# A decoder layer with a mixture of experts on one core: a second gather buffer at expert 0, and the last expert's rows added by TensorE

## The reference

```python
out, new_a, new_b, v = token_mixer(x, ...)
h = layer_norm(ALPHA * x + out, ln1_g, ln1_b)
# moe_ffn(h): router, then
for e in range(N_EXPERTS):                       # 16 experts, 1024 -> 512 -> 1024
    u = jax.nn.silu(t @ w_gate[e]) * (t @ w_up[e])
    out = out + gates[:, e:e + 1] * (u @ w_down[e])   # gates: 2 non-zero per token
y = layer_norm(ALPHA * h + f, ln2_g, ln2_b)
```

## Time and profile before

| | us |
|---|---|
| median of 3 runs | 1049.32 (1045.19 to 1050.66) |
| the profiled execution | 1048.14 |
| its span, first to last instruction | 1046.4 |
| mean granted TensorE clock | 0.978 |
| TensorE busy | 995.1 (95%) |
| VectorE busy | 792.4 (76%) |
| ScalarE busy | 473.1 (45%) |
| GpSimd busy | 372.4 (36%) |
| moved by DMA | 190.52 MB, mean 182 GB/s |

### The profile page before, as it was taken

How to read it: one execution, slowest core, us unless ns; L and a number is a source line. 1 busy time by engine, 2 the same in 40 slices (tenths; PEclk the granted TensorE clock), 3 DMA queues, 4 the chain that set the end, 5 groups by cost and what they waited for, 6 DMA issues and landing times.

```text
span 1046.4 us, 19478 instructions
## 1 busy us (share of the span) xinstructions
PE 995.1 (95%) x7212; PEld 901.5 (86%) x7212; DVE 792.4 (76%) x965; ACT 473.1 (45%) x665; POOL 372.4 (36%) x275
## 2 busy tenths in 40 slices
PE   7999999999999999999999999995999999999980
PEld 7999999999999998999999999974677777777760
DVE  2698889888999995744434598147789898999986
ACT  4232222323232244334442323424678787878763
POOL 2444434444544770445454544410110000000362
PEclk9999999999999999999999999997899999999995
DMA  7433232323232221333235534548899999999574
GB/s 220 122 93 95 85 100 81 100 80 100 81 101 81 80 82 49 100 110 89 81 99 170 172 90 144 208 163 317 300 368 391 375 391 379 383 388 393 203 253 165
DMA packets 163400, 190.52 MB, mean 182 GB/s; under 512 B 6675, under 2 KB 114195, under 8 KB 163340
## 3 DMA queue, kind: packets, MB, share of 16 engines
q1 hardware_dynamic: 156619, 177.65, 49.8%
q0 software_dynamic: 3008, 10.55, 3.2%
q10 hardware_dynamic: 3729, 1.75, 0.7%
HBM read 179.16 MB, written 11.76 MB: 182 GB/s over the span
## 4 chain that ended last, share of the span: by engine, by line
PE 57%; issue 25%; POOL 12%; DVE 3%; DMA 2%; ACT 1%; POOLq 0%; DVEq 0%
PE pr L986 27%; PE pr L1172 16%; POOL w_lo L562 12%; PE work L1172 8%; PE work L1148 1%; DMA hs<-h_rows,ids 1%; PE work L1069 1%; PE pr L1198 1%; DVE w_gate_lo L1625 1%; PE pr L1088 1%; PE work L1191 1%; DMA y_b<-y_rows,slot_b 1%; DVE y_a L1793 0%; PE work L1096 0%; DVE y_b L1789 0%
## 5 line engine op out<-in xcount | busy, mean ns | idle before, releaser
L562 POOL TENSOR_TENSOR w_lo<-raw,w_hi 128x512 fp32r<-128x512 f32 x208 | 298.0, 1453 | 334.5 <-ACT w_hi L680 334.5
L986 PE MATMUL pr<-x_hi,w_hi 128*128 128x260 f32 x1264 | 255.0, 283 | 0.2 <-POOL w_lo L562 0.2
L986 PE MATMUL pr<-x_hi,w_lo 128*128 128x260 f32 x1264 | 254.7, 283 | 0.0
L986 PE MATMUL pr<-x_lo,w_hi 128*128 128x260 f32 x1264 | 254.3, 283 | 0.0
L684 ACT ACTIVATE ev<-pr 128x520 f32<-128x520 f32 x96 | 58.1, 605 | 375.1 <-PE pr L986 375.1
L986 PEld LDWEIGHTS pr<-x_hi,w_hi 128*128 128x128 f32 x1264 | 195.0, 189 | 0.5 <-POOL w_lo L562 0.4
L986 PEld LDWEIGHTS pr<-x_hi,w_lo 128*128 128x128 f32 x1264 | 195.0, 188 | 0.0
L986 PEld LDWEIGHTS pr<-x_lo,w_hi 128*128 128x128 f32 x1264 | 194.4, 188 | 0.0
L1355 DVE SCALAR_TENSOR_TENSOR work<-b_pad,par,work 128x512 f32<-128x512 f32 x224 | 148.2, 743 | 0.0
L680 ACT ACTIVATE w_hi<-raw 128x512 fp32r<-128x512 f32 x208 | 118.9, 623 | 4.9 <-DMA raw<-in_w_in_dram 2.6
L599 POOL DMA_INDIRECT hs<-h_rows,ids x16 | 20.2, 1260 | 256.4 <-DVE ids L1619 246.6
(11 more groups left out here) (337 smaller groups left out, 1704.5 us busy)
## 6 DMA issues: line engine op xcount, KB each, us to landing
raw<-in_w_in_dram SPq DMA_DIRECT2D x80, 512.0 KB, 3.7
w_gate<-in_expert_w_gate_dram SPq DMA_DIRECT2D x16, 2048.0 KB, 14.9
w_up<-in_expert_w_up_dram SPq DMA_DIRECT2D x16, 2048.0 KB, 14.3
w_down<-in_expert_w_down_dram SPq DMA_DIRECT2D x16, 2048.0 KB, 13.6
y_rows<-y_out SPq DMA_DIRECT2D x15, 384.0 KB, 13.1
raw<-in_w_a_out_dram SPq DMA_DIRECT2D x8, 512.0 KB, 3.6
raw<-in_w_c_out_dram SPq DMA_DIRECT2D x8, 512.0 KB, 3.7
raw<-in_w_b_out_dram SPq DMA_DIRECT2D x8, 512.0 KB, 3.6
```

Source lines behind the costliest of these rows:

```text
L562: pool.tensor_tensor(w_lo[:, slot, k], raw[:, slot, k], w_hi[:, slot, k].bitcast(F32), ALU.subtract).then_inc(w_split, 1)
L986: mm = pe.matmul(pr[slot][:, h, 0:HALF], w[:, slot, k, :], x[:, k, h * HALF:(h + 1) * HALF], start=(k == 0 and w is w_hi and x is hi), sto ...
```

## The change

Two edits that had been made apart are joined.

*At expert 0.* A second buffer `hs_second` takes the gather of expert 1's rows (`gather_second`), which waits for the row numbers alone; `turn` reads it once. Gate of slot 2 is loaded ahead of `h_out`, and "up" of slot 2 and "down" of slots 1 and 2 are held back until the second gather has landed. 30 idle transposes stand ahead of TensorE's wait for `mb`; `keep_busy` issues 18 and 8 in place of 20 and 12.

*At the end.* `share_marks` makes a 96x128 matrix for each block of 128 tokens: the weight of the last expert's row for each token that has one. TensorE transposes it between the two halves of the last "down", and `share_last` computes, in PSUM, `y_a` (times the identity, float32) plus this matrix times the last expert's rows, in three products of parts. ScalarE and VectorE split the matrix and the rows. `slot_ready` sends a token whose second expert is the last to another row, with weight `s_wm` zero. GpSimd so fetches `y_b` after all stores of `y_out`, and only the samples wait for the last halves. `summed_up` adds `y_b` in PSUM. For blocks 0 to 2 the final pass is split: ScalarE scales (`scaled`), GpSimd adds the bias row (`shifted`) and the block leaves from `y_b`; block 3 is finished by VectorE in two halves and sent by ScalarE. The branch is turned round, so that the path taken stands first, with its own copy of the end.

```diff
@@ SyncE, before expert_pass
             expert_load(first, 0, TURN[0], "down")
+            expert_load(first, 2, TURN[2], "gate")
             h_out()
-            expert_load(first, 2, TURN[2], "gate")
+            sp.wait_ge(second_in, 16)
             expert_load(first, 2, TURN[2], "up")
-            sp.wait_ge(first.gathered, 16)
             expert_load(first, 1, TURN[1], "down")
             expert_load(first, 2, TURN[2], "down")
@@ GpSimd
+            def gather_second():
+                pool.wait_ge(first.ids_ready, 3)
+                pool.indirect_dma_start(out=hs_second[:], out_offset=None, in_=h_rows,
+                                        in_offset=bass.IndirectOffsetOnAxis(ap=ids[:, 1:2], axis=0)).then_inc(second_in, 16)
+            def shifted():
+                for b in range(3):
+                    pool.wait_ge(std2_ready, (5, 8, 11)[b])
+                    pool.tensor_tensor(y_b[:, b, :], y_a[:, b, :], ln2_rows[:, 1, :], ALU.add).then_inc(added, 1)
-                pool.wait_ge(first.half_stored, 32)
-                fetch(y_b, slot_b, y_b_in, y_rows[0:E * C, :])
+                pool.wait_ge(slots_ready, 4)
+                pool.wait_ge(first.stored, 16 * E)
+                fetch(y_b, slot_ready, y_b_in, y_rows[0:(E - 1) * C, :])
+                pool.wait_ge(first.half_stored, 32)
+                fetch_samples(sy_b, 2, y_b_in, y_rows[0:E * C, :])
+                shifted()
@@ ScalarE, last_rows_out
                     act.activation(y_last[:, cols], work[0][0:C, h, :], ACT.Copy).then_inc(ps.half_ready, 1)
+                    if ps is first:
+                        if h == 0:
+                            act.wait_ge(end_mm, 2)
+                            act.activation(share_hi[:], pr[1][0:C, 1, :], ACT.Copy).then_inc(end_act, 1)
+                        act.activation(y_last_hi[:, cols], work[0][0:C, h, :], ACT.Copy).then_inc(end_act, 1)
@@ ScalarE, the end
+            def scaled(b):
+                act.wait_ge(var_ready, (3, 5, 7)[b])
+                act.activation(y_a[:, b, :], y_a[:, b, :], ACT.Copy, scale=agg[:, b % 2, 3:4]).then_inc(std2_ready, 1)
+                deviation(0)
+                deviation(1)
+                scaled(0)
...
+                deviation(2)
+                scaled(1)
...
+                deviation(3)
+                scaled(2)
@@ TensorE
+            for _ in range(30):
+                pe.transpose(pr[0][:, 1, 0:P], ident[:], ident[:])
             pe.wait_ge(mb_ready, 1)
...
-                    keep_busy(20)
+                    keep_busy(18)
                 turn(ps, n0)
                 if ps is first:
-                    keep_busy(12)
+                    keep_busy(8)
...
+                down_last(ps, t, 0)
+                if ps is first:
+                    pe.wait_ge(end_dve, 3)
+                    for b in range(4):
+                        mm = pe.transpose(pr[1][0:C, 1, b * P:(b + 1) * P], share_tok[:, b, :], ident[:])
+                    mm.then_inc(end_mm, 1)
+                down_last(ps, t, 1)
+                    pe.matmul(z_tile[b][:, h, :], ident[:], y_a[:, b, cols], start=True, stop=False)
+                    for w, y in ((share_hi, y_last_hi), (share_lo, y_last_hi), (share_hi, y_last_lo)):
+                        mm = pe.matmul(z_tile[b][:, h, :], w[:, n], y[:, cols], start=False, stop=y is y_last_lo)
@@ VectorE
+                do(dve.tensor_tensor(share_tok[:], share_tok[:], rep(s_wb[:, 0:4], 2, C), ALU.mult), to_end)
...
+                partial(0, landed)
+                dve.wait_ge(end_act, 1)
+                dve.tensor_tensor(share_lo[:], pr[1][0:C, 1, :], share_hi[:].bitcast(F32), ALU.subtract).then_inc(end_dve, 1)
+                share_low(0)
+                partial(1, landed)
+                share_low(1)
+                partial(2, landed)
```

More of the change, by code:

```diff
@@ L511, in _, with results_out @@
             expert_pass(first, 0, 0)
+            def results_out():
+                for b in range(2):
+                    sp.wait_ge(added, b + 1)
+                    sp.dma_start(y_prompt[0, b * P:(b + 1) * P, :], y_b[:, b, :]).then_inc(fin_out[0], 16)
+                sp.wait_ge(fin_ready, 1)
+                sp.dma_start(y_sample[:, 0, :].rearrange("s (c f) -> (s c) f", f=CS), sy_a).then_inc(fin_out[0], 16)
+                sp.wait_ge(added, 3)
+                sp.dma_start(y_prompt[0, 2 * P:3 * P, :], y_b[:, 2, :]).then_inc(fin_out[0], 16)
             n_max = further_passes(sp)
-            with sp.If(n_max > C):
+            with sp.If(n_max < C + 1):
+                results_out()
+            with sp.Else():
                 sp.wait_ge(first.stored, 16 * E)
@@ L530, in _ @@
                 sp.sem_inc(y_read, 1)
[L531 to L540, removed]
+                results_out()
+            sp.wait_ge(fin_out[0], 64)
             sp.wait_ge(fin_out[1], 32)
@@ L606, in step @@
                     t = e + n0
-                    if m == 0:
+                    if m == 0 and ps is first:
+                        gather_second()
+                    elif m == 0:
                         gather(ps, 1, t + 1)
@@ L663, in _ @@
                 fetch_samples(sy_b, 2, y_b_in, y_rows)
-            with pool.Else():
-                pool.wait_ge(first.stored, 16 * E)
-                pool.wait_ge(first.half_stored, 32)
-                fetch(y_b, slot_b, y_b_in, y_rows[0:E * C, :])
-                fetch_samples(sy_b, 2, y_b_in, y_rows[0:E * C, :])
+                shifted()
         @block.scalar
@@ L1143, in find_ids, with turn @@
                 mm.then_inc(ps.ids_mm, 1)
-            def turn(ps, t):
-                pe.wait_ge(ps.gathered, t * 16 + 16)
+            def turn(ps, t, second=False, late=16):
+                source = hs
+                if second:
+                    source = hs_second
+                    pe.wait_ge(second_in, 16)
+                else:
+                    pe.wait_ge(ps.gathered, t * 16 + late)
                 for k in range(KB):
-                    mm = pe.transpose(work[0][:, k // 4, k % 4 * C:(k % 4 + 1) * C], hs[:, k * P:(k + 1) * P], ident[0:C, 0:C])
+                    mm = pe.transpose(work[0][:, k // 4, k % 4 * C:(k % 4 + 1) * C], source[:, k * P:(k + 1) * P], ident[0:C, 0:C])
                 mm.then_inc(ps.turned, 1)
@@ L1223, in step @@
                     if m < 15:
-                        turn(ps, t + 1)
+                        turn(ps, t + 1, second=ps is first and m == 0, late=0 if ps is first else 16)
                     product(ps, "up", s, t, x_hi_t, x_lo_t, lambda h: pr[0][0:C, 1, :], 1)
@@ new lines, in partials, with partials_late @@
+            def partials(landed):
+                dve.wait_ge(back_in, 32)
+                partial(0, landed)
[5 more added lines that the diff above has]
+                partial(2, landed)
+            def partials_late():
+                partial(3, 16)
+                sample_partial(16)
@@ L1758, in _ @@
             expert_pass(first, 0)
-            dve.wait_ge(back_in, 32)
-            partials(16)
+            counts = (chain.n, to_var.n, to_fin.n, to_slots.n)
             n_max = further_passes(dve)
-            with dve.If(n_max > C):
+            with dve.If(n_max < C + 1):
+                dve.wait_ge(ln_in, 16 * 2 * (TS + 1))
+                results(partials_late)
+            chain.n, to_var.n, to_fin.n, to_slots.n = counts
+            with dve.Else():
                 dve.sem_inc(further.ids_ready, 1)
                 dve.sem_inc(further.u_ready, 1)
+                partials_late()
                 dve.wait_ge(first.half_ready, 2)
```

233 lines of the change are left out of this document (152 added, 81 removed).

## The result

| | median, us | runs | ratio to before | 95% interval |
|---|---|---|---|---|
| kernel before, same chip | 1046.72 | 10 | 1 | |
| changed kernel | 1052.16 | 10 | 1.0046 | 1.0030 to 1.0062 |
| changed kernel, second series | 1052.27 | 12 | 1.0033 | 1.0018 to 1.0048 |

The profiled execution took 1052.15 us, its span 1050.4 us (before: 1048.14 and 1046.4). The forecast was -1.6 us against the profiled execution; +4.0 came. The time lies inside the range that I gave, but a slight gain was forecast and a small loss was measured: both intervals lie above 1.

The account below looks back on a forecast made before the run. Bound: the chain through the second gather, then TensorE with DMA nearly full, then the tail. Start and experts 5.9 + 0.3 - 2.5 - 3.1 - 1.1 = -0.5, tail 2.1: 1.6 us gained, median 1047.7 us, range 1041.0 to 1053.5.

Parts of the forecast that it names:

- the range that I gave: Whole kernel: measured time between 1041.0 and 1053.5 us.
- a slight gain: Whole kernel: 1.6 us off the profiled execution, to 1046.5 us; 1047.7 us as median.
- a stretch in which the tie had hardly begun: Expert stage: three intervals up to 977 us gave steps of 18.17 us, costing 3.1 us over 11 stores.
- the slack: Expert stage: 2.05 us before TensorE needs VectorE's low part of `u`, called the tightest; TensorE then loses 2.5 us.

Follow-up runs that it names:

- second profile: The profile of the whole change run once more, unaltered; that series measured 1.0033 of the kernel before (1052.27 us).

## What to carry to other kernels

Before bringing work forward in a stage whose DMA engines are full, list what shares a queue with the transfer that somebody awaits; a small awaited store belongs in a queue without bulk loads, or ahead of them. In a stage tied to transfers take the average step from bytes over measured rate (18.4 us here, where four profiles gave 18.27 to 18.40), not from a stretch in which the tie had hardly begun. And to find the slack, go through every product that an engine reads, the small ones too: an instruction of 0.65 us placed behind two long ones was the tight edge, and moving it was worth nothing or 8 us depending on what else bound.

## What the runs showed of the hardware

- An issue on a queue can itself be long. SyncE's issue of a load took 0.37 us as a rule in the kernel before. In the changed one it took 7.02 us at 754.84 us, when three earlier loads had not landed (they landed at 759.97, 765.23 and 772.38; the issue ended at 761.86); what stands behind it, a ready store too, waits. GpSimd's issue of the same store took 0.56 us and ScalarE's 0.32. In the kernel with its stores in GpSimd's queue the issue of an "up" load took 8.9 us (median of 12), and nothing waited for it. What limits the issue was not tried.
- Taking the awaited store out of the ring left the total rate at 385 GB/s and made loads slower to land (the one of a gate near 949 us 22.4 us instead of 18.7).
- A pause of TensorE of 5.67 us was followed by 1.2 GHz until 790 us; one of 3.65 us by a mean granted clock of 0.72 from 784 to 790 us. In "up" the first cost 1.9 us; in the second profile a pause of 5.62 us cost 0.6 there.
- GpSimd's issue of an indirect fetch of `y_b` took 0.94 us, but 2.55 beside a VectorE pass with two SBUF inputs (L1859), and ended 0.81 us after that pass did (1023.73 + 1.27 = 1025.00; 1025.81). In the kernel with its stores in GpSimd's queue the second fetch met the same pass (until 1014.52), took 1.38 and ended 0.82 us after it (1015.34):

```profile
1013.96 1.38 POOL L666 DMA_INDIRECT y_b<-y_rows,slot_ready  x1 [0.30 <-issue]
...
1013.25 1.27 DVE L1867 SCALAR_TENSOR_TENSOR y_a<-y_a,s,h_back 128x1024 f32<-128x1024 f32 x1
```

  The Trainium skill (SBUF — State Buffer, Who interferes with whom) has an instruction of GpSimd that reads SBUF shut out of the port that it shares with VectorE for the whole of such a pass. That would fit both, if reading the row numbers counts; the same section infers that the making of descriptors needs only the write side, which such a pass leaves free. Two fetches of `y_a` in the changed kernel show the pattern too: issued beside VectorE's low parts of "down" (both inputs in SBUF) they took 2.41 and 2.56 us and ended 0.82 and 0.83 us after the passes (1011.64 after 1010.82, 1014.51 after 1013.68). It reaches the total: in the three profiles of the new tail whose first fetch of `y_b` took 2.5 us, the stretch from rows_out of expert 14 to the end took 34.1 to 34.8 us, in the other six 32.2 to 33.6. That the pass is the cause was seen side by side and not tested.
